# Decay factors of a gated delta rule: exponents from 32-row products of turned running sums and indicators instead of full-height products, with a rectifier on ScalarE

## The reference, cut to what matters

```python
gam = jnp.cumsum(g, axis=-1)                       # running sum of the log decays in a chunk
diff = gam[..., :, None] - gam[..., None, :]
Lmat = jnp.exp(jnp.where(incl, diff, -jnp.inf))
kb = k * beta[..., None]
A = jnp.where(strict, jnp.einsum('bhntk,bhnsk->bhnts', kb, k) * Lmat, 0.0)
T = triangular_solve(eye + A, eye)                 # lower, unit diagonal
qk = jnp.einsum('bhntk,bhnsk->bhnts', q, k) * Lmat
```

## Time and profile before

| | us |
|---|---|
| median of three runs (lowest, highest) | 2571.73 (2570.83, 2573.20) |
| the profiled execution | 2572.86 |
| its span in the profile | 2571.0 |
| TensorE busy | 2515.2 |
| VectorE busy | 1315.1 |
| ScalarE busy | 657.7 |

### The profile page before, as it was taken

The page is one execution under the profiler, slowest core; times in us unless marked ns, Lnnn a source line. Parts: engine busy times, 40 slices in busy tenths (PEclk is TensorE's granted clock), DMA queues, the critical chain, the costliest instruction groups (busy, mean ns, idle before and its releaser), DMA issues.

```text
span 2571.0 us, 30831 instructions
## 1 busy us (share of the span) xinstructions
PE 2515.2 (98%) x12547; PEld 1703.3 (66%) x12547; DVE 1315.1 (51%) x2507; ACT 657.7 (26%) x1486; POOL 60.1 (2%) x116
## 2 busy tenths in 40 slices
PE   8999999999999999999999999999999999999999
PEld 4477567555788888645545745555555876888886
DVE  6765352653544465335454365747483444344564
ACT  2133232363300000223433052534433002000001
POOL 0000000000000000000000010101020000000000
PEclk9999999999999999999999999999999999999999
DMA  4111222101222322211111311211122312322221
GB/s 161 66 66 66 91 75 86 34 33 54 78 79 86 98 75 82 90 66 67 66 67 47 119 62 37 82 66 50 66 73 92 137 68 66 98 86 78 98 82 66
DMA packets 121028, 196.81 MB, mean 77 GB/s; under 512 B 5212, under 2 KB 61336, under 8 KB 119992
## 3 DMA queue, kind: packets, MB, share of 16 engines
q1 hardware_dynamic: 118848, 180.52, 20.7%
q0 software_dynamic: 1344, 12.19, 1.2%
q10 hardware_dynamic: 696, 2.13, 0.2%
HBM read 187.49 MB, written 7.34 MB: 76 GB/s over the span
## 4 chain that ended last, share of the span: by engine, by line
PE 94%; DVE 3%; ACT 2%; issue 1%; DMA 0%; ACTq 0%; SPq 0%; DVEq 0%
PE psum L547 22%; PE psum L544 16%; PE psum L2539 9%; PE psum L2521 9%; PE psum L423 7%; PE psum L408 6%; PE psum L449 4%; PE psum L2574 4%; PE psum L473 2%; PE psum L1240 2%; PE psum L466 1%; PE psum L396 1%; PE psum L1234 1%; PE psum L1255 1%; PE psum L2465 1%
## 5 line engine op out<-in xcount | busy, mean ns | idle before, releaser
L600 DVE TENSOR_TENSOR arena<-arena,psum 128x512 f32<-128x512 f32 x197 | 135.1, 686 | 353.2 <-PE psum L547 301.8
L2521 PE MATMUL psum<-h_t,weight_ring 128*128 128x512 f32 x576 | 264.0, 598 | 0.3 <-issue 0.3
L2539 PE MATMUL psum<-weight_ring,h_t 128*128 128x512 f32 x576 | 256.7, 598 | 1.9 <-ACT arena L2871 1.4
L547 PE MATMUL psum<-h_t,weight_ring 128*128 128x256 f32 x1120 | 250.2, 379 | 1.2 <-DVE h_t L741 1.0
L547 PEld LDWEIGHTS psum<-h_t,weight_ring 128*128 128x128 f32 x1120 | 212.4, 190 | 30.9 <-issue 2.2
L544 PE MATMUL psum<-weight_ring,arena 128*128 128x256 f32 x992 | 220.5, 379 | 1.5 <-ACT arena L2999 1.5
L544 PEld LDWEIGHTS psum<-weight_ring,arena 128*128 128x128 f32 x992 | 188.3, 190 | 27.9 <-issue 2.4
L2539 PEld LDWEIGHTS psum<-weight_ring,h_t 128*128 128x128 f32 x576 | 107.2, 191 | 128.7 <-issue 125.6
L423 PE MATMUL psum<-h_t,weight_ring 128*128 128x512 f32 x416 | 181.8, 598 | 0.5 <-issue 0.5
L2521 PEld LDWEIGHTS psum<-h_t,weight_ring 128*128 128x128 f32 x576 | 105.2, 191 | 107.5 <-issue 105.2
L547 PE MATMUL psum<-arena 128*128 128x256 f32 x768 | 169.7, 379 | 0.0
(11 more groups left out here) (459 smaller groups left out, 3293.3 us busy)
## 6 DMA issues: line engine op xcount, KB each, us to landing
weight_ring<-in_ffn_w_in_dram SPq DMA_DIRECT2D x44, 1024.0 KB, 7.4
weight_ring<-in_w_in_dram SPq DMA_DIRECT2D x20, 2048.0 KB, 7.8
weight_ring<-in_ffn_w_out_dram SPq DMA_DIRECT2D x8, 2048.0 KB, 8.1
weight_ring<-in_w_in_even_dram SPq DMA_DIRECT2D x7, 2048.0 KB, 8.1
weight_ring<-in_w_in_odd_dram SPq DMA_DIRECT2D x5, 2048.0 KB, 7.9
weight_ring<-in_w_in_dram SPq DMA_DIRECT2D x8, 1024.0 KB, 6.8
weight_ring<-in_w_branch_gdn_dram SPq DMA_DIRECT2D x4, 2048.0 KB, 7.8
weight_ring<-in_ffn_w_out_dram SPq DMA_DIRECT2D x4, 1536.0 KB, 6.6
```

The lines of the kernel that those rows point to most:

```text
L547: ins = pe.matmul(out, w, right[:, k, :], start=first, stop=last)
L600: ins = dve.tensor_tensor(out, other, bank, op)
L2521: last = pe.matmul(bank, slot[:, k, n * P:(n + 1) * P], act[:, k, :], start=(k == 0), stop=(k == KD - 1))
L2539: last = pe.matmul(bank, act[:, k, t * P:(t + 1) * P], slot[:, k, :], start=(k == 0), stop=(k == KD - 1))
```

## The change

Running sums are turned once: eight products per program, in four pairs, give for each group g a 128x128 tile `gam_t` whose 32 rows from 32j belong to chunk j. In them rows 0 to 3 hold the four heads' running sums over the tokens, and rows 16 to 19 the negated ones plus the logarithm of beta (clamped at 1e-37). TensorE makes them in one bank, behind the lead of 16 and ahead of the first group; ScalarE copies the bank to SBUF in `act_gdn`, between the first and the second padded feature, and logs of beta are taken on ScalarE in the step before.

For each group VectorE then makes two sides from `gam_t` with per-row factors and addends from a constant table `slots` (five instructions on 128x128), and TensorE multiplies 32 rows by 32 rows for each chunk, 128x512 results: the four chunks use the four row groups and four banks, one after the other with no other work between. ScalarE reads each result with Relu of the negated value and takes Exp of the negated result. The multiplication by beta and the four triangles times rates on VectorE go. The decays have four places instead of two: two in `decay`, two in `z`, which is free until the gates are written. The heads of a chunk are stored in another order (`head_place`).

```diff
 def pe_gdn(...):
     pe_take(fill, FIRST_LEAD)
+    pe.wait_ge(K.rates_spread, 1)
+    bank = pe_fresh(K, pe, (s, "gam_t"))
+    rates, logs = (V["spread"][:, n].rearrange("p g j c -> p g (j c)") for n in range(2))
+    for g in range(4):
+        pe.matmul(bank[:, g * P:(g + 1) * P], rates[:, g, :], K.const("cum"), start=True, stop=False)
+        last = pe.matmul(bank[:, g * P:(g + 1) * P], logs[:, g, :], K.const("ident"), start=False, stop=True)
+    last.then_inc(K.full_of((s, "gam_t")), 1)
 def pe_gdn_prepare(...):
+    pe_gdn_decays(K, pe, s, V, g)
     for pair in ((0, 1), (2, 3)):
-        pe_gdn_decays(K, pe, s, V, g, pair)
         pe.wait_ge(K.unit_vectors, 4 * g + 4)
-def pe_gdn_decays(K, pe, s, V, g, tiles):
-    for j in tiles:
-        pe.wait_ge(K.cum_scaled, NT * g + j + 1)
-        bank = pe_fresh(K, pe, (s, "diff", g, j))
-        pe.matmul(bank, K.const("after"), V["cums"][:, j % 2, :], start=True, stop=True).then_inc(K.full_of((s, "diff", g, j)), 1)
+def pe_gdn_decays(K, pe, s, V, g):
+    pe.wait_ge(K.decay_sides, g + 1)
+    banks = [pe_fresh(K, pe, (s, "diff", g, j)) for j in range(NT)]
+    for j in range(NT):
+        rows = slice(32 * j, 32 * j + 32)
+        pe.matmul(banks[j], V["gam_t"][rows, g, :], V["heads_t"][rows].rearrange("p v t -> p (v t)"), start=True,
+                  stop=True).then_inc(K.full_of((s, "diff", g, j)), 1)
 def act_gdn(K, act, s, V):
     for n in range(5):
+        if n == 1:
+            act.wait_ge(K.full_of(key), K.turn(key))
+            act.copy(V["gam_t"].rearrange("p g t -> p (g t)"), K.bank(key)).then_inc(K.free_of(key), 1)
         if n < 4:
             act_gdn_pad(K, act, s, V, 0, n)
         if n:
             act_gdn_conv_silu(K, act, s, V, 0, n - 1)
             act_gdn_square(K, act, s, V, 0, n - 1)
 def act_gdn_decay(K, act, s, V, g, j):
-    act.activation(V["decay"][:, j % 2, :], K.bank((s, "diff", g, j)), ACT.Exp).then_inc(K.free_of((s, "diff", g, j)), 1)
+    act.activation(decay, K.bank((s, "diff", g, j)), ACT.Relu, scale=-1.0).then_inc(K.free_of((s, "diff", g, j)), 1)
+    act.wait_ge(K.free_of((s, "diff", g, j)), K.turn((s, "diff", g, j)))
+    act.activation(decay, decay, ACT.Exp, scale=-1.0).then_inc(K.decays_ready, 1)
 def dve_gdn(K, dve, s, V):
+    dve.memset(V["masked"], 0.0).then_inc(K.one_more("dve"), 1)
 def dve_gdn_products(K, dve, s, V, g, j):
-    dve.tensor_tensor(decay, decay, beta, ALU.mult).then_inc(K.one_more("dve"), 1)
```

## The result

| | kernel before | changed kernel |
|---|---|---|
| median, us | 2571.19 | 2578.16 |
| lowest to highest, of 10 runs each | 2570.10 to 2573.20 | 2576.54 to 2579.92 |
| the profiled execution | 2572.86 | 2579.52 |
| its span | 2571.0 | 2577.7 |

The account below looks back on a forecast made before the run. TensorE, 98% busy, was taken to bound the kernel. First group 13.1 us more (14.2 at the entry, less 0.6 and 0.5), later groups 3.5 less: 9.6 slower, median 2581.3, range 2573 to 2587.

Parts of the forecast that it names:

- the entry wait: First group: ScalarE's in-order copy of the turned sums delays the squares TensorE needs; fill 10.8 us later at full clock.
- The clock at the entry: After TensorE's hole before the first group, a low clock adds 0.9 us for the last sum, 2.5 for the fill.
- The second sum: First group's sums on TensorE: taken as squares come, the last begun at 1516.0; no bank wait foreseen.
- The rest of the first group: After the entry: 0.6 us less around the decays and 0.5 less at the later wait for silu.
- Tile 5: First group's fill after the key products waits for ScalarE to read this tile, after Relu and Exp: 1.1 us more.
- Row groups: Each group's four 32-row products on TensorE run side by side, 1.26 us with changes of shape.
- Rival C: The four 32-row products don't overlap: 3.64 us a group instead of 1.26, 9.5 more, 2590.8; chance 5%.
- Groups two to four: Decays there: 3.44 us goes, 1.26 plus a 1.0 wait comes; 1.2 less each, 3.5 in all.
- bank wait: Groups two to four: TensorE wants four banks before ScalarE has copied the second turned output; 1.0 us each.
- Rival D: Relu needs its own table, so each Relu and Exp pair on ScalarE loads twice: 2590 to 2610; chance 3%.
- A: Not slower: ScalarE is not held at its copy of the turned sums; 2568.9, or 2566 without bank waits; chance 7%.
- B: Wait at the entry comes at full clock, bank waits in groups two to four don't: 2573 to 2575; chance 9%.

Follow-up runs that it names:

- experiments 1: Changed kernel with the turned sums ahead of the lead of 16 on TensorE instead of behind it: 2569.19 us.
- experiment 3: Changed kernel with only ScalarE's copy of the turned sums moved behind the four features of the first group: 2570.72 us.
- Experiment 4: Changed kernel with eight unread full-height products put behind the turned sums, where TensorE stands still: 2578.11 us.
- experiment 7: Changed kernel with a short unread full-height product between each two of the four 32-row products, so none run side by side: 2607.25 us.
- experiment 5: Changed kernel with two filling products of groups two to four moved between the turned outputs and the decays: 2575.13 us.
- experiment 10: Changed kernel with earlier turned sums, moved fill and earlier tile 5 (2564.20 us), plus four unread 32-row products ahead of each group's decays: 2581.03 us.
- experiment 11: Changed kernel with earlier turned sums, moved fill and earlier tile 5 (2564.20 us), plus four unread full-height products ahead of each group's decays: 2577.81 us.

## Why the prediction was right, point by point

- **What decides.** Right: the entry wait, not the arithmetic. The hole, ScalarE's idle and the torn block of sums stand in the trace as named, and experiments 1 and 3 give the time back from TensorE's side and from ScalarE's.
- **Its size.** The fill was to start 10.8 later at full clock; it does so 10.9 later. ScalarE's copy was put at 1504.6 and is at 1504.8; the last square was to end at 1515.95 and ends at 1516.05.
- **The clock at the entry.** The one mis-sized term. I added 0.9 for the last sum and 2.5 for the fill. The clock did fall, for 6.8 us, but the stretch ended at 1515.8, before the last sum. What was slow before that was slow inside a wait. Experiment 4, which takes the low clock away, changes the median by 0.05 us. I had kept 0 as the other end, but for another reason, that the clock might not fall; that the lower price came is in this part luck. The step that failed is that I gave the low stretch a length and no start. In the earlier trace rows TensorE had been all but still since 1528.0 when the low stretch began at 1532.8. The hole opened at about 1504.6, so an estimate from that one row, which is no rule, starts the low stretch near 1509.4 and, with 3.4 to 6.8 us, ends it between 1512.8 and 1516.2, ahead of the fill. It was 1509.0 to 1515.8.
- **The second sum.** I had TensorE take its sums as squares come. The second one waited for the bank of the fourth feature, a wait that I didn't have; it lay inside the wait for the last square.
- **The rest of the first group.** Tile 5: 1.1 more predicted, 12.2 - 11.1 = 1.1 measured. The whole from the decays to the turned values: 1.1 less predicted, 1.4 less measured (11.1 against 9.75).
- **Row groups.** 1.26 predicted for four products with their changes of shape. In the trace they take 1.14, from 1524.23 to 1525.37, and 1.07 in the second group (1644.81 to 1645.88), and experiment 7 shows what they cost one by one. Rival C is out.
- **Groups two to four.** 3.5 less predicted, 9.75 - 6.54 = 3.2 measured, with a bank wait of 0.97 in each where I had 1.0; experiment 5 gives 3.0 us for the three.
- **Relu.** No table load, so Rival D is out. The Trainium skill's statement (ScalarE: Activation LUTs, Table sets: the hidden batching unit) that relu is in every set agrees with this trace.
- **The sum.** 11.1 - 1.4 - 3.2 = 6.5 at the end of the stage, 6.7 between the profiled executions, 7.0 between the medians; predicted 9.6, and without the 3.4 for the clock 6.2.
- **Rivals A and B.** A needed ScalarE free at the entry; experiment 3 builds that and lands at 2570.7, near A's 2568.9. B was to have no bank waits, and they came; its other half, an entry at the price of full clock, is what was measured.

## What to carry to other kernels

A result that one engine reads early in its in-order program must be made as early on the engine that makes it: ask of each new wait what stands behind it, not how long its own work is. If an engine has a lead of filler, place small products that others wait for ahead of it, and spend filler only up to the point where the wait is covered; here four products of the lead were worth 5.7 us elsewhere. Here the four row groups wrote to four banks and asked for all of them at once, and that cost 0.97 us a group until the banks' readers had more time, so look at who still has to read them.

## What the runs showed of the hardware

- The granted clock fell behind a stretch in which the profile has TensorE busy all the time, with products of 32 rows one after the other and short full-height ones between: 5.00 busy of 5.00 us, then 0.50 for 3.4 us (experiment 7, first group), and in or behind the three like it. With 32-row products alone it fell inside one of four stretches (experiment 10), with full-height products at the same place in none (experiment 11), in one profiled execution each. Behind four row groups at once, 1.14 us in a stretch, no profiled execution shows a fall.
- A low clock inside a wait costs nothing that the medians can measure: 6.8 us at 0.50 against none, 2578.16 and 2578.11 (experiment 4). Where it lasted past the wait, in experiment 5's execution, the next work started 0.65 us later.
- The scatter of the changed kernel's executions goes with the clock: of the ten, the two fastest (2576.54 and 2576.86) have a mean granted clock of 0.996, the other eight 0.995.
- Four 32-row float32 products of 512 columns in four row groups and four banks take 1.07 to 1.14 us together; alone each takes 1.05 between two changes of shape.
